# Norms between the stages of a two-layer decoder step: statistics with tokens on partitions, spread by TensorE, and two results per row in the first items

## The reference, cut to what matters

```python
def rms_norm(x, g):
    xf = x.astype(jnp.float32)
    y = xf * lax.rsqrt(jnp.mean(xf * xf, axis=-1, keepdims=True) + EPS)
    return y.astype(x.dtype) * g
...
        hp = rms_norm(yp, norm2_g[i]) * (1.0 + sc2p) + sh2p
        hs = rms_norm(ys, norm2_g[i]) * (1.0 + sc2s) + sh2s
        yp = yp + g2p * swiglu(hp, ffn_w_gu[i], ffn_w_down[i])
...
def swiglu(h, w_gu, w_down):
    g, u = jnp.split(h @ w_gu, 2, axis=-1)
    return (jax.nn.silu(g) * u) @ w_down
```

## Time and profile before

| | |
|---|---|
| median of 3 runs | 2644.62 us (2642.03 to 2655.07) |
| span of the profiled execution | 2645.1 us; no time of its own outside the span is shown |
| TensorE busy, mean clock granted | 95%, 0.982 of full |
| VectorE, ScalarE, GpSimd busy | 68%, 43%, 49% |
| boundary 0 | about 766 to 864 us |
| boundary 1 | about 1506 to 1589 us |
| boundary 2 | about 1884 to 1968 us |

### The profile page before, as it was taken

One profiled execution on the slowest core, in us unless ns is written; L12 is line 12 of the kernel. 1 busy time (PEld: TensorE's weight loads), 2 busy tenths in 40 slices (PEclk: granted clock), 3 DMA queues, 4 the chain that ended last, 5 costly groups with the idle time before them and its releaser, 6 DMA issues.

```text
span 2645.1 us, 51365 instructions
## 1 busy us (share of the span) xinstructions
PE 2503.9 (95%) x20020; PEld 2304.4 (87%) x20020; DVE 1797.7 (68%) x3095; ACT 1127.1 (43%) x2070; POOL 1286.0 (49%) x973
## 2 busy tenths in 40 slices
PE   5979999999998999999999989999889999999999
PEld 4847864677898999999999989999889999999998
DVE  6388988665248666656667687767695665656775
ACT  5155656775135444444212363332454444442223
POOL 2403652443135656556544535545355656555444
PEclk8999999999899999999999999999999999999999
DMA  9205557202334444344985233328324434369731
GB/s 321 78 22 160 174 206 254 63 2 81 114 102 113 139 130 162 122 152 143 342 328 183 97 97 106 106 90 328 100 85 150 155 117 161 126 210 364 288 131 70
DMA packets 316388, 407.98 MB, mean 154 GB/s; under 512 B 40816, under 2 KB 227032, under 8 KB 313338
## 3 DMA queue, kind: packets, MB, share of 16 engines
q1 hardware_dynamic: 316154, 404.75, 45.7%
HBM read 284.85 MB, written 119.85 MB: 153 GB/s over the span
## 4 chain that ended last, share of the span: by engine, by line
PE 65%; DVE 15%; DMA 6%; issue 5%; POOL 4%; ACT 3%; SPq 2%; DVEq 0%; ACTq 0%; POOLq 0%
PE PS L589 9%; PE PS L2456 9%; PE PS L2458 9%; PE PS L2457 9%; PE PS L2500 5%; PE PS L2502 5%; PE PS L2503 5%; PE PS L1835 3%; PE PS L1864 2%; PE PS L1846 2%; DMA t_scratch<-stage 2%; POOL ring L2775 2%; DMA a_scratch<-stage 1%; DVE s_all L1532 1%; POOL stage L2788 1%
## 5 line engine op out<-in xcount | busy, mean ns | idle before, releaser
L2456 PE MATMUL PS<-th,ring 128*128 128x264 f32 x2800 | 802.7, 287 | 28.0 <-DVE y L2920 9.4
L2458 PE MATMUL PS<-th,ring 128*128 128x264 f32 x2800 | 798.7, 285 | 0.0
L2457 PE MATMUL PS<-th,ring 128*128 128x264 f32 x2800 | 797.9, 285 | 0.0
L2456 PEld LDWEIGHTS PS<-th,ring 128*128 128x128 f32 x2800 | 529.9, 189 | 35.4 <-issue 30.3
L2457 PEld LDWEIGHTS PS<-th,ring 128*128 128x128 f32 x2800 | 530.1, 189 | 0.0
L2458 PEld LDWEIGHTS PS<-th,ring 128*128 128x128 f32 x2800 | 530.1, 189 | 0.0
L2775 POOL TENSOR_TENSOR ring<-wraw,ring 128x512 fp32r<-128x512 f32 x232 | 339.5, 1468 | 359.9 <-ACT ring L2579 359.3
L2775 POOL TENSOR_TENSOR ring<-sums,ring 128x512 fp32r<-128x512 f32 x216 | 319.9, 1483 | 284.0 <-ACT ring L2579 283.8
L2500 PE MATMUL PS<-th,ring 128*128 128x264 f32 x1232 | 352.4, 286 | 13.6 <-DVE zs L3089 6.4
L2502 PE MATMUL PS<-th,ring 128*128 128x264 f32 x1232 | 351.2, 285 | 0.0
L2503 PE MATMUL PS<-th,ring 128*128 128x264 f32 x1232 | 350.7, 285 | 0.0
(11 more groups left out here) (371 smaller groups left out, 5187.4 us busy)
## 6 DMA issues: line engine op xcount, KB each, us to landing
t_scratch<-stage SPq DMA_DIRECT2D x154, 528.0 KB, 3.4
th<-t_scratch SPq DMA_DIRECT2D x77, 1056.0 KB, 8.8
wraw<-in_ffn_w_gu_dram SPq DMA_DIRECT2D x96, 512.0 KB, 5.2
wraw<-in_ada_w_dram SPq DMA_DIRECT2D x80, 512.0 KB, 4.9
wraw<-in_ffn_w_down_dram SPq DMA_DIRECT2D x80, 256.0 KB, 6.0
wraw<-in_conv_w_in_dram SPq DMA_DIRECT2D x28, 512.0 KB, 5.2
y<-y_scratch SPq DMA_DIRECT2D x12, 1056.0 KB, 8.7
y_scratch<-y SPq DMA_DIRECT2D x6, 2112.0 KB, 8.2
```

The costliest lines, as they stand in the source:

```text
L2456: pe.matmul(out, hi, x[:, TH, k, :], start=(k == 0 and i in (1, 2, 5)), stop=False, skip_group_check=True)
L2457: pe.matmul(out, hi, x[:, TL, k, :], start=False, stop=False, skip_group_check=True)
L2458: last = pe.matmul(out, lo, x[:, TH, k, :], start=False, stop=(k == 3), skip_group_check=True)
```

## The change

- Statistics: instead of a matrix of ones times the 528 summed columns, the sums are the weights: six blocks of 88 tokens, each times one column of ones, so that the means stand in PSUM with tokens on 88 partitions and 6 columns (`pe_stats`). The square of the last row isn't added by GpSimd; it is a second, accumulating matmul for each block (12 in all). Mean, root and reciprocal are on 88x6.
- Spread: VectorE multiplies the identity by the reciprocal roots into an 88x528 array of six diagonal blocks, and TensorE multiplies ones by it (`pe_broadcast`, 512 and 16 columns), so that banks 4 and 5 (group 0) or 6 and 7 (group 1) hold the root in every partition. The row products read it from there.
- Order: the statistics of group 1 stand behind the whole item (g,0), the spread behind the first four blocks of (u,0). For group 0 the spread stands two units (or one item) behind the statistics. On ScalarE the table of the root is asked for ahead (`act_root_ahead`), and the root comes before more of the squares.
- The "gc" items go through the rows side by side: result 0 with row ft, then result 1 with row ft - 2. Their ring slots come free in another order: blocks 0 and 2 at a new semaphore after block (1,3), blocks 1 and 3 with the results. ScalarE's order in these items is now: split, take, split, take, then both build steps, then two splits.
- VectorE's order around the last units of the stage before is shifted by one to two units.

The diff, cut to its core:

```diff
@@ -189,6 +189,8 @@
                 SLOT[len(PREP)] = len(RING)
                 RING.append(len(PREP))
                 DONE.append(_res + {"U": _pos + 1, "C": _pos // 2 + 1, "D": 2 * _pos + 2, "P": 8 + 8 * (_pos // 2)}[_stage])
+                if _stage == "C" and _kind in "gc":
+                    DONE[-1] = _res + 1 + _pos // 2 if _pos % 2 else None
...
+AD0 = [0, 6, 12, 18, 24, 30, 36, 43]
+NBLK, BLK = 6, GS // 6
+FRESH = [it.n for it in ITEMS if it.stage == "C" and it.kind in "gc"]
...
             for k in range(16, 24):
                 pe_out_item(pe, k)
                 if k == 16:
-                    pe_sum(pe, 0, 0)
+                    pe_stats(pe, 0, 0)
+                if k == 17:
+                    pe_broadcast(pe, 0, 0)
...
             act_square(act, 0, 0, 7)
+            act_root_ahead(act)
             split_hi(act, "out", KT, MM0["out"] + 17)
+            act_root(act, 0, 0)
             act_square(act, 0, 1, 0)
-            act_root(act, 0, 0)
             split_hi(act, "out", KT + 1, MM0["out"] + 18)
             act_square(act, 0, 1, 1)
...
-            for i in range(1, KT):
+            for i in range(1, KT - 1):
                 pool_add(pool, 0, 0, i)
             split_lo(pool, "out", KT)
...
             dve_out_item(dve, 16)
             dve_mean(dve, 0, 0)
-            dve_recip(dve, 0, 0, 0)
-            dve_recip(dve, 0, 0, 1)
+            dve_recip(dve, 0, 0)
+            dve_out_item(dve, 17)
             dve_row(dve, 0, 0, 0)
             dve_row(dve, 0, 0, 1)
-            dve_out_item(dve, 17)
...
+            if f in (1, 2) and s == 0 and i == KT - 1:
+                return tA[:, 0, :]
...
+        def stat_of(f, s):
+            return hx[0:BLK, 12, GS:GS + NBLK] if f == 0 and s == 0 else st6[0:BLK, s, 0:NBLK]
+        def diag_of(f, s):
+            return hx[0:BLK, 12, 0:GS] if f == 0 and s == 0 else rs2[0:BLK, s, :]
+        def rstd_of(s):
+            return wide(4 + 2 * s)[:, 0:GS]
+        def means_at(s, w=BLK):
+            return PS[0:w, 5 + 2 * s, 400:400 + NBLK]
...
-            for mi in range(2):
-                r = it.res + mi
-                pe_bank_free(pe, r)
-                for b in range(2):
-                    p = it.prep + 2 * mi + b
-                    w = slot_of(p)
+            for mi, ft in side_by_side() if fresh else itertools.product(range(2), range(KT)):
+                b, k = divmod(ft, 4)
+                r, p = it.res + mi, it.prep + 2 * mi + b
+                w = slot_of(p)
+                if ft == 0:
+                    pe_bank_free(pe, r)
+                if k == 0:
                     pe_split_ready(pe, p)
-                    for k in range(4):
-                        if fresh and mi == 0:
-                            pe.wait_ge(n_lop, row_lo(f, s, 4 * b + k))
-                        hi, lo = w[:, RH, P * k:P * k + P], w[:, RL, P * k:P * k + P]
-                        for h in range(2):
-                            out, x = PS[:, 2 * SET[r] + h, 0:H], th[s][:, :, (T_AT[1], T_AT[2])[b] + h]
-                            pe.matmul(out, hi, x[:, TH, k, :], start=(b == 0 and k == 0), stop=False, skip_group_check=True)
-                            pe.matmul(out, hi, x[:, TL, k, :], start=False, stop=False, skip_group_check=True)
-                            last = pe.matmul(out, lo, x[:, TH, k, :], start=False, stop=(b == 1 and k == 3), skip_group_check=True)
-                last.then_inc(r_mm, 1)
-                if fresh and s == 0 and mi == 0:
-                    pe_sum(pe, f, 1)
+                if fresh and mi == 0:
+                    pe.wait_ge(n_lop, row_lo(f, s, ft))
+                hi, lo = w[:, RH, P * k:P * k + P], w[:, RL, P * k:P * k + P]
+                for h in range(2):
+                    out, x = PS[:, 2 * SET[r] + h, 0:H], th[s][:, :, (T_AT[1], T_AT[2])[b] + h]
+                    pe.matmul(out, hi, x[:, TH, k, :], start=(ft == 0), stop=False, skip_group_check=True)
+                    pe.matmul(out, hi, x[:, TL, k, :], start=False, stop=False, skip_group_check=True)
+                    last = pe.matmul(out, lo, x[:, TH, k, :], start=False, stop=(ft == 7), skip_group_check=True)
+                if ft == 7:
+                    last.then_inc(r_mm, 1)
+                elif fresh and (mi, ft) == (1, 3):
+                    last.then_inc(c_mm, 1)
+                if not fresh and s == 0 and (mi, ft) == (0, 3):
+                    pe_broadcast(pe, f, 1)
+            if fresh and s == 0:
+                pe_stats(pe, f, 1)
+        def side_by_side():
+            for ft in range(KT + 2):
+                if ft < KT:
+                    yield 0, ft
+                if ft >= 2:
+                    yield 1, ft - 2
...
-        def pe_sum(pe, f, s):
+        def pe_stats(pe, f, s):
 
             g = 2 * f + s
-            pe.wait_ge(n_ad, 7 * g + 7)
+            pe.wait_ge(n_ad, AD0[g] + 6)
+            pe.wait_ge(n_sq, SQ0[g] + 8)
             if f and s:
                 pe.wait_ge(n_rd, f)
             after(pe, n_ms, g)
-            acc = acc_of(f, s)
-            for h in range(2):
-                last = pe.matmul(PS[:, 4 + h, 0:H], ones[:], acc[:, H * h:H * h + H], start=True, stop=True)
+            acc, tail = acc_of(f, s), square_of(f, s, KT - 1)
+            for j in range(NBLK):
+                w = min(BLK, prompt_cols(f, s) - BLK * j)
+                pe.matmul(means_at(s)[:, j:j + 1], acc[:, BLK * j:BLK * j + BLK], ones[:, 0:1], start=True, stop=False,
+                          skip_group_check=True)
+                last = pe.matmul(means_at(s, w)[:, j:j + 1], tail[:, BLK * j:BLK * j + w], ones[:, 0:1], start=False, stop=True,
+                                 skip_group_check=True)
             last.then_inc(n_sum, 1)
+        def pe_broadcast(pe, f, s):
+            pe.wait_ge(n_rs, 2 * (2 * f + s) + 2)
+            for c in (slice(0, 512), slice(512, GS)):
+                last = pe.matmul(rstd_of(s)[:, c], ones[0:BLK, :], diag_of(f, s)[:, c], start=True, stop=True)
+            last.then_inc(n_bc, 1)
...
                 pe_plain(pe, Z_ITEM[f], u)
                 if f < 2 and u == 9:
-                    pe_sum(pe, f + 1, 0)
+                    pe_stats(pe, f + 1, 0)
+                if f < 2 and u == 11:
+                    pe_broadcast(pe, f + 1, 0)
...
+            elif DONE[SLOT[p] - 4] is None:
+                act.wait_ge(c_mm, FRESH.index(PREP[RING[SLOT[p] - 4]][0]) + 2)
...
+            if it.kind in "gc":
+                for mi in range(2):
+                    act_split(act, PREP_AT[it.n, mi])
+                    act_c_take(act, it, mi)
+                act_c_build(act, it.phase, step)
+                act_c_build(act, it.phase, step + 1)
+                for pos in (2, 3):
+                    act_split(act, PREP_AT[it.n, pos])
+                return
...
         def act_root(act, f, s):
             act.wait_ge(n_ms, 2 * f + s + 1)
-            act.activation(rstd_of(f, s), rstd_of(f, s), ACT.Sqrt).then_inc(n_rt, 1)
+            act.activation(stat_of(f, s), stat_of(f, s), ACT.Sqrt).then_inc(n_rt, 1)
+        def act_root_ahead(act):
+            act.activation(st6[:, 3, 0:1], ones[:, 0:1], ACT.Sqrt)
...
-            for i in range(3):
-                act_square(act, g, 1, i)
+            act_square(act, g, 1, 0)
             act_root(act, g, 0)
-            for i in (3, 4, 5):
+            for i in (1, 2, 3):
                 act_square(act, g, 1, i)
             for ft in range(8):
                 act_row(act, g, 0, ft)
-                if ft in (3, 5):
-                    act_square(act, g, 1, 6 if ft == 3 else 7)
+                if ft in (1, 2, 3, 5):
+                    act_square(act, g, 1, 4 + (1, 2, 3, 5).index(ft))
...
-            for i in range(1, 6):
+            for i in range(1, 7):
                 pool_add(pool, g, 1, i)
-            pool_add(pool, g, 1, 6)
-            pool_add(pool, g, 1, 7)
...
-                dve.wait_ge(n_rs, 2 * (2 * f + s) + 2)
+                dve.wait_ge(n_bc, 2 * f + s + 1)
             if s:
                 dve.tensor_copy(v[:, w:GS], zs[:, ft, :])
-            dve.tensor_tensor(v[:, 0:w], y[:, ft, GS * s:GS * s + w], rstd_of(f, s)[:, 0:w], ALU.mult).then_inc(n_x, 1)
+            dve.tensor_tensor(v[:, 0:w], y[:, ft, GS * s:GS * s + w], rstd_of(s)[:, 0:w], ALU.mult).then_inc(n_x, 1)
 
...
                 dve_mean(dve, f, 1)
-                dve_recip(dve, f, 1, 0)
-                dve_recip(dve, f, 1, 1)
+                dve_recip(dve, f, 1)
...
-            dve.tensor_scalar(rstd_of(f, s).rearrange("p (h n) -> p h n", h=2), PS[:, 4:6, 0:H], 1.0 / D, EPS, ALU.mult, ALU.add)\
-                .then_inc(n_ms, 1)
-
-        def dve_recip(dve, f, s, h):
-            dve.wait_ge(n_rt, 2 * f + s + 1)
-            v = rstd_of(f, s)[:, H * h:H * h + H]
+            dve.tensor_scalar(stat_of(f, s), means_at(s), 1.0 / D, EPS, ALU.mult, ALU.add).then_inc(n_ms, 1)
+        def dve_recip(dve, f, s):
```

(21 more changed lines are left out.)

22 lines of the change are left out of this document (11 added, 11 removed).

## The result

| | before | after |
|---|---|---|
| median of 12 runs each | 2649.22 us (2642.03 to 2655.07) | 2656.52 us (2650.51 to 2662.63) |
| ratio, 95% interval | | 1.0034 (1.0024 to 1.0044), that is +9 us |
| span of the profiled execution | 2645.1 us | 2650.6 us, of one that took 2652.49 |

The medians lie 7.3 us apart, the ratio says 9 us (6.4 to 11.7): a small loss, but the interval leaves out zero. An execution's time is 1.7 to 2.5 us more than its span, in all kernels alike, so there is time outside the span; the change leaves it as it is.

A forecast was written before the change was run, and what follows sets the result against it. VectorE's chain from the sample products to the take that frees a bank was taken to set each boundary's end. Boundaries of 5.6, 3.2 and 2.8 us, together 11.6, on 2644.62 gave 2656 us, range 2634 to 2668.

The forecast's parts named there:

- S: Start of the sample products, VectorE's first work behind the second group's root; forecast at E + 6.7.
- E: End of the first group's first item on TensorE; forecast at 812.8 us in boundary 0, 1533.5 in boundary 1.
- Where S lands: In boundaries 0, 1 and 2, S was to come 2.1 us later, 1.2 us sooner and 1.0 us sooner.
- Rows: The eight rows behind S, last low row in, end at S + 16.1, not S + 17.8: 1.7 us won.
- TensorE's wait: In the second group's first item, TensorE does three blocks by S + 12, then waits nearly 6 us for position 2 weights.
- The clock: Behind TensorE's wait, one stretch at halved clock over about 15 matmuls costs 1.5 us.
- Rival (c): More than one stretch at halved clock in each boundary, and statistics at 3.0 us: 11 us more, 2667 us; chance 0.15.
- High sums: ScalarE does them after both takes, ending the first at S + 30.5; VectorE stands still 5.5 and 6.9 us before low sum 6.
- Given back: GpSimd's next two splits fall into VectorE's stall, so one low sum meets a split; ends 3.5 or 4.4 us later.
- Rival (a): High sums are not late, as position 2 weights come in time or low rows are slower: -8 us, 2637 us; chance 0.15.
- Rival (b): The first item's end decides, not VectorE's chain behind S: 2622 us; chance 0.07.
- Rival (d): The order does nothing that reaches the end: 2645 us; chance 0.08.

The follow-up runs named there:

- experiment 1: The changed kernel with ScalarE's four high sums of group 0 ahead of the two takes: 2640.45 us, ratio 0.9972.
- two profiles: The kernel before, unchanged, was profiled a second time: one time of 2647.74 us, profiled span 2646.0 us.
- 3: The kernel before with the new statistics and spread alone, old order of products, ring releases and ScalarE's order: 2637.70 us, ratio 0.9965.
- 4: The kernel before with the new order alone, old statistics, second group's sum behind the whole first item: 2671.39 us, ratio 1.0088.
- 6: The kernel of experiment 1 with the second group's statistics moved into the first group's item: 2636.51 us, ratio 0.9957.
- 7: Kernel 3 with ScalarE's rows 0 and 1 of the second group ahead of its second take: 2639.90 us, ratio 0.9968.
- 11: The changed kernel with high sums ahead of the takes and the spread behind two blocks instead of four: 2635.47 us, ratio 0.9951.
- 10: The changed kernel with side by side in the first group only and the spread behind two blocks: 2633.50 us, ratio 0.9942.
- 2: The changed kernel with side by side in the first group only, old order in the second: 2639.98 us, ratio 0.9973.
- 5: Kernel 2 with the second group's statistics inside the first group's item and ScalarE's root ahead of the takes: 2637.16 us, ratio 0.9957.
- 8: The changed kernel with the second group's spread behind two blocks instead of four: 2653.25 us, ratio 1.0022.
- 9: The changed kernel with the second group's spread behind eight blocks instead of four: 2668.36 us, ratio 1.0065.

## Why the prediction was right

Forecast 2656, measured 2656.5. That the two agree to half a microsecond is luck: the forecast added 11.6 us to 2644.62, the median of three runs, and the median of twelve is 2649.22, from which the same sum gives 2661. What can be compared is the difference: +11.6 forecast, +9.0 measured (6.4 to 11.7).

The mechanism was the predicted one, and experiment 1 shows it. With VectorE's pause removed, the loss is gone and more: 16 us, where the prediction put 12 to 18 on the absence of the pause. Inside the sum some terms were off and partly made up for each other. The steps one by one:

- **Statistics.** 1.97 us for a forecast of 2.6 with its tail; mean, root and reciprocal 0.16 to 0.21 us, the diagonal 0.70, the spread 1.2 us to VectorE's start, all as forecast. S stands at E + 6.0 for E + 6.7 (E = 805.8).
- **Where S lands.** Against before: boundary 0 +1.4 us on the mean of two profiles (forecast +2.1), boundary 1 -2.9 (forecast -1.2), boundary 2 -2.7 (forecast -1.0). The term that was mis-sized most is the first group's item: in boundary 1 it ended at 1532.7 for a forecast of 1533.5, it had no halved stretch (0.6 us were set aside), and the statistics took 0.6 us less.
- **Rows.** The last low row ends at S + 15.95 in each boundary, forecast S + 16.1; in the first profile of before it was S + 17.9 in boundaries 0 and 1. The prediction's own terms for it (0.3 us sooner, 1.1 us shorter) make only 1.4 of its 1.7 us.
- **TensorE's wait.** Forecast: one of nearly 6 us behind three blocks. Measured: 2.28 us ahead of the item, for VectorE's take of the result before (L3040, which stands between VectorE's rows), then 2.14 us behind three blocks for the ring. This step was wrong in kind: the first wait was not counted. It did no harm to the sum, since the end of the second wait is set by the weights and not by TensorE: they are ready at S + 17.2 (forecast 17.8).
- **The clock.** One halved stretch was forecast behind that wait. There are two: behind the 2.28 us the matmuls start 0.22 us apart for 16 in a row, and again from 830.0, one microsecond into the work behind the second wait. The first costs nothing at the end, since TensorE then waits for the weights all the same. Rival (c) had more than one halved stretch, but put the other into the first group's item; its statistics of 3.0 us and its price did not come. The stretch 823.0 to 826.8 (PEclk, third from last, is 0.55: 1.2 of 2.4 GHz for nearly all of it) and TensorE's timeline from 829.83:

```profile
823.00:826.80 3.80, 3.80 (x18) 3.66 (x18) 3.11 (x7) 3.28 (x6) 0.00 (x0) 0.55 0.00 0
```

```profile
829.83 0.30 PE L2498 MATMUL PS<-th,ring 128*128 128x264 f32 x1
829.95 0.40 PE L2499 MATMUL PS<-th,ring 128*128 128x264 f32 x1
830.14 0.42 PE L2500 MATMUL PS<-th,ring 128*128 128x264 f32 x1
830.37 0.42 PE L2498 MATMUL PS<-th,ring 128*128 128x264 f32 x1
```

- **High sums.** VectorE's low sum 6 at S + 30.15 in boundary 0 and S + 30.2 in boundary 1, forecast S + 30.5. VectorE stood still for 7.25 and 8.55 us, forecast 5.5 and 6.9: its rows and operands were done sooner than I had them.
- **Given back.** The four low sums in the changed kernel take 1.25 us each, none of them lengthened (forecast: one). In boundary 0 GpSimd's next two splits begin at 845.43, with the last low sum at 845.45; there it is the splits that are longer, 4.66 us for the two where two take 2.74 elsewhere (808.76). From S to the end of the boundary 49.9, 51.4 and 51.4 us against 47.5 (mean of two), 46.9 and 47.5: +2.4, +4.5 and +3.9 for +3.5, +4.4 and +3.8.
- **The sum.** The boundaries have grown by 3.8, 1.6 and 1.1 us on the means of before, 6.6 us, where 11.6 was forecast; 4.1 of the 5.0 us between are S. Two slips of arithmetic are in the forecast: 799.1 + 1.8 + 0.85 - 0.55 is 801.2 and not 801.0, and 819.5 is 2.2 us behind 817.29 and not 2.1. Put right, S lands 2.3 us later in boundary 0, and the sum is 11.8.
- **What is left.** The time has grown by 9 us and the boundaries by 6.6, which is inside the interval (6.4 to 11.7). Kernels 3, 4, 6, 7 and 11 agree with their column "later" within 1.4 us, the others within 3.7; 10 gains 2.6 us more in time than there, and 1, 2, 5, 8, 9 and the changed kernel come out 2.4 to 3.7 us worse. From boundary 0 to 1 every kernel but the one before takes 643.0 to 647.2 us, the two profiles of before 641.9 and 643.8. That may be scatter or a cost of the changed code; it was not tried, and stays open.
- **PSUM as a source.** VectorE's row product now reads PSUM. Its group in the whole span, against 709 ns out of SBUF:

```profile
L3050 DVE TENSOR_TENSOR xf<-y,PS 128x528 f32<-128x528 f32 x24 | 16.4, 696 | 1.3 <-PE PS L2591 1.2
```

It costs nothing, as the prediction had it. The Trainium skill (VectorE: DVE Perf Modes, the section on the TRN2 errata) would have a larger fixed term for a PSUM source; this row shows none.

Rival (a), high sums not late, did not happen in the changed kernel, but kernel 1 makes it happen: 7.4 us faster than before, where (a) was priced at 8. Rival (b) needed pauses of VectorE behind S. There were such pauses, but they hung on ScalarE's list and so followed S. Rival (d), no effect at the end, falls by the interval, which leaves out 1, and by experiments 3 and 4: two effects, -9 and +23 us, of which the result is what is left.
